# Stick breaking with features on the partitions: one product turned round, the outputs' transposes left out

## What is computed

```
u = rmsnorm(x) @ w_in            # queries qb, keys kb, values vb, gate zb: 1024 columns each
z = (q @ k^T) / sqrt(128)        # per head, per block of 128 queries, keys up to the block
log_1mb = where(s < t, log_sigmoid(-z), 0)
A = where(s < t, exp(log_sigmoid(z) + sum over s < j < t of log_1mb), 0)
hb = A @ v
yb = hb * silu(zb)
y = concat(ya, yb) @ w_out       # ya: the mLSTM branch
x = x + rmsnorm(y)
```

## Time and profile before

| | |
|---|---|
| median of 3 runs | 1892.0 us |
| lowest, highest | 1891.76, 1892.29 us |
| profiled execution, own time | 1892.71 us |
| its span | 1890.7 us |
| mean granted TensorE clock | 0.999 of full speed |
| TensorE busy in the span | 99% |

### The profile page before, as it was taken

The page is one execution under the profiler, slowest core; times in us unless marked ns, Lnnn a source line. Parts: engine busy times, 40 slices in busy tenths (PEclk is TensorE's granted clock), DMA queues, the critical chain, the costliest instruction groups (busy, mean ns, idle before and its releaser), DMA issues.

```text
span 1890.7 us, 25969 instructions
## 1 busy us (share of the span) xinstructions
PE 1877.7 (99%) x9298; PEld 1589.8 (84%) x9298; DVE 1000.3 (53%) x1489; ACT 899.3 (48%) x1737; POOL 1043.7 (55%) x1265
## 2 busy tenths in 40 slices
PE   9999999999999999999999999999999999999998
PEld 7878888898888988888889888888878888998887
DVE  2531321431123398777737864876546748854652
ACT  5522443532333454455555544276646756653332
POOL 5732644453465498878854753166524364565572
PEclk9999999999999999999999999999999999999999
DMA  6341533232233432233242331569522244733331
GB/s 238 103 110 43 136 84 89 73 87 75 78 106 106 146 100 90 90 111 109 74 146 62 105 96 45 134 173 273 127 62 68 95 140 121 192 102 94 95 117 50
DMA packets 112626, 205.52 MB, mean 109 GB/s; under 512 B 11612, under 2 KB 17352, under 8 KB 112510
## 3 DMA queue, kind: packets, MB, share of 16 engines
q1 hardware_dynamic: 97684, 176.70, 31.0%
q0 software_dynamic: 6912, 12.59, 4.1%
q10 hardware_dynamic: 7914, 14.69, 2.3%
HBM read 195.80 MB, written 8.12 MB: 108 GB/s over the span
## 4 chain that ended last, share of the span: by engine, by line
PE 96%; DVE 2%; ACT 1%; DMA 0%; issue 0%; POOL 0%; DVEq 0%; SPq 0%; ACTq 0%; POOLq 0%
PE proj L2664 22%; PE proj L2666 21%; PE proj L2665 21%; PE work L3100 2%; PE work L3102 2%; PE work L3101 2%; PE proj L2822 2%; PE proj L2821 2%; PE proj L2823 2%; PE proj L2815 1%; PE proj L2817 1%; PE proj L2818 1%; PE work L3262 1%; PE work L2666 1%; PE work L2665 1%; PE work L2664 1%
## 5 line engine op out<-in xcount | busy, mean ns | idle before, releaser
L788 POOL TENSOR_TENSOR w_lo<-w_raw,w_hi 128x256 fp32r<-128x256 f32 x1008 | 821.4, 850 | 684.5 <-ACT w_hi L862 683.9
L862 ACT CAST w_hi<-w_raw 128x512 fp32r<-128x512 f32 x552 | 326.4, 619 | 402.1 <-PE proj L2666 309.0
L2664 PE MATMUL proj<-act_hi,w_hi 128*128 128x512 f32 (+1 forms) x1184 | 446.9, 377 | 0.6 <-DVE arena L1970 0.3
L2666 PE MATMUL proj<-act_hi,w_lo 128*128 128x512 f32 (+1 forms) x1184 | 440.7, 372 | 0.0
L2665 PE MATMUL proj<-act_lo,w_hi 128*128 128x512 f32 (+1 forms) x1184 | 440.5, 372 | 0.0
L2664 PEld LDWEIGHTS proj<-act_hi,w_hi 128*128 128x128 f32 x1184 | 223.1, 188 | 40.2 <-issue 0.7
L2665 PEld LDWEIGHTS proj<-act_lo,w_hi 128*128 128x128 f32 x1184 | 223.1, 188 | 39.1 <-issue 0.7
L2666 PEld LDWEIGHTS proj<-act_hi,w_lo 128*128 128x128 f32 x1184 | 222.9, 188 | 39.2
L2664 PE MATMUL proj<-w_hi,act_hi 128*128 128x512 f32 x512 | 203.8, 398 | 0.1
L788 POOL TENSOR_TENSOR w_lo<-arena,w_hi 128x256 fp32r<-128x256 f32 x188 | 174.6, 962 | 48.6 <-ACT w_hi L862 48.5
L2666 PE MATMUL proj<-w_hi,act_lo 128*128 128x512 f32 x512 | 200.1, 391 | 0.0
(11 more groups left out here) (436 smaller groups left out, 3259.1 us busy)
## 6 DMA issues: line engine op xcount, KB each, us to landing
w_raw<-in_w_in SPq DMA_DIRECT2D x154, 256.0 KB, 2.7
w_raw<-in_w_in_ab SPq DMA_DIRECT2D x130, 256.0 KB, 2.8
w_raw<-in_w_mlp SPq DMA_DIRECT2D x72, 256.0 KB, 2.9
arena<-in_w_mlp SPq DMA_DIRECT2D x28, 512.0 KB, 4.0
w_raw<-in_w_in_c SPq DMA_DIRECT2D x56, 256.0 KB, 2.9
arena<-in_w_in_ab SPq DMA_DIRECT2D x32, 256.0 KB, 4.3
w_raw<-in_w_out_ab SPq DMA_DIRECT2D x32, 256.0 KB, 2.6
w_raw<-in_w_out_c SPq DMA_DIRECT2D x32, 256.0 KB, 2.7
```

What stands on the lines that cost most here:

```text
L788: ins = pool.tensor_tensor(w_lo[:, slot, c], raw_of(b)[:, c], w_hi[:, slot, c].bitcast(F32), ALU.subtract)
L862: act.copy(w_hi[:, b % RING, :], raw_of(b)).then_inc(hi_ready, 1)
L2664: pe.matmul(out_, a_hi, b_hi, start=first, stop=False, skip_group_check=by_part)
L2666: return pe.matmul(out_, a_lo, b_hi, start=False, stop=last, skip_group_check=by_part)
```

## The change

- `sb_z` is computed with features on the partitions, as the odd layer's slabs are. Its quarters leave PSUM by VectorE (`rowed`: times the row of token scales), and ScalarE applies silu in place in SBUF to two banks at a time, waits for it and sends them to DRAM (`gate_spilled`), each a step later in ScalarE's program. The DRAM tensor is now feature by token.
- `values` has its operands swapped: its output has features on the partitions, and `sb_o` with it. The eight `turn_tile` and their waits go.
- `fill_hi` and `fill_lo` for the output's second half read `sb_o` in SBUF. ScalarE makes five of the eight in step 32 and three in step 33, VectorE seven in step 33 and the last behind the loop.
- `scores` waits, at the first unit of each head, for that head's keys alone.
- `GATED_AT` is one step later throughout.

```diff
--- before.py
+++ after.py
@@ -453 @@
...
-        sb_v, sb_o = [view(12288, MT, SEQ), view(14336, MT, SEQ)], view(0, MT, D)
+        sb_v, sb_o = [view(12288, MT, SEQ), view(14336, MT, SEQ)], view(0, KD, SEQ)
...
@@ -465 @@
...
-        gate_dram = nc.dram_tensor("gate_made", (SEQ, D), F32, kind="Internal").ap().rearrange("(m p) d -> p m d", p=P)
+        gate_dram = nc.dram_tensor("gate_made", (D, SEQ), F32, kind="Internal").ap().rearrange("(k p) t -> p k t", p=P)
...
@@ -1399 @@
 
             o_, spilled_, z_, v_ = even_sevens
 
-            def spill(quarter):
-                at, tokens, i = sevens.index(spilled_), (0, 2, 0, 2)[quarter], (0, 1, 1, 0)[quarter]
+            def gate_spilled(quarter):
+                at, half, i = sevens.index(spilled_), (0, 1, 0, 1)[quarter], (0, 1, 1, 0)[quarter]
+                slots = (late_gates if quarter > 1 else gate_tmp)[:, 2 * (quarter % 2):2 * (quarter % 2) + 2, :]
                 if quarter == 0:
                     act.wait_ge(a_out, 2 * at + 2)
                 elif quarter == 1:
                     act.wait_ge(own_out, 2 * at + 2)
                 else:
                     act.wait_ge(proj_free, spilled_.bank0 + 2 * (quarter - 2) + 2)
-                slot = 2 * (quarter % 2)
-                act.dma_start(gate_dram[:, tokens:tokens + 2, i * NCOL:(i + 1) * NCOL], (late_gates if quarter > 1 else gate_tmp)[:, slot:slot + 2, :])\
-                   .then_inc(dram_spilled, 16)
+                step(act.activation(slots, slots, ACT.Silu))
+                act.dma_start(gate_dram[:, 4 * i:4 * i + 4, 2 * P * half:2 * P * (half + 1)],
+                              slots.rearrange("p m (c t) -> p (m c) t", c=2)).then_inc(dram_spilled, 16)
...
@@ -1477 @@
             act.activation(root[:], stat[:], ACT.Sqrt, bias=eps_col[:, 0:1], scale=4.0 / D).then_inc(head_root_ready, 1)
             act.preload_act_table_set("silu_and_others")
             prepared_to(spilled_, B22, 3)
-            gate(spilled_, 0, ACT.Silu, None)
-            spill(0)
             prepared_to(spilled_, T4, 3)
-            gate(spilled_, 1, ACT.Silu, None)
-            spill(1)
+            gate_spilled(0)
             prepared_to(z_, B11, 3)
-            gate(spilled_, 2, ACT.Silu, None)
-            spill(2)
+            gate_spilled(1)
             prepared_to(z_, T1, 3)
-            gate(spilled_, 3, ACT.Silu, None)
-            spill(3)
+            gate_spilled(2)
             prepared_to(z_, T2, 3)
+            gate_spilled(3)
...
@@ -1547 @@
             def gates_back():
                 act.wait_ge(dram_spilled, 32 + 16 * 4)
                 act.wait_ge(sb_z_full, SB_UNITS // 2)
-                act.dma_start(first_gate, gate_dram[:, :, 0:NCOL]).then_inc(dram_returned, 16)
+                act.dma_start(first_gate, gate_dram[:, 0:4, :]).then_inc(dram_returned, 16)
                 act.wait_ge(sb_o_full, SB_UNITS // 2)
-                act.dma_start(sb_gate, gate_dram[:, :, NCOL:D]).then_inc(dram_returned, 16)
+                act.dma_start(sb_gate, gate_dram[:, 4:8, :]).then_inc(dram_returned, 16)
...
@@ -1564 @@
                     weights(i - 1)
                 if i == SB_UNITS // 2 + 2:
                     gates_back()
+                if i == SB_UNITS:
+                    fill_hi("act", ACT_AT["yb"], 5, src=sb_o, ready=(yb_ready, lambda k: k + 1), after=end("sb_k"))
+                if i == SB_UNITS + 1:
+                    fill_hi("act", ACT_AT["yb"], KD, src=sb_o, ready=(sb_o_copied, lambda k: MT * (k + 1)), k0=5)
                 for s, j in [x_ for later in beside[i:i + 3] for x_ in later]:
                     prepare(s.first + j + 1)
             ahead(by_name["even_out0"][1])
-            fill_hi("act", ACT_AT["yb"], 2, turn=TURN_AT["yb"], after=end("sb_k"))
             act.wait_ge(sb_o_copied, SB_UNITS)
             for r in range(2):
                 act.dma_start(post_row[r], bass.AP(W["post_norm_g_2"].tensor, r * D, [[0, P], [1, D]]))\
                    .then_inc(rows_loaded, 16)
             act.dma_start(pre1_row, bass.AP(W["pre_norm_g_2"].tensor, D, [[0, P], [1, D]])).then_inc(rows_loaded, 16)
-            fill_hi("act", ACT_AT["yb"], KD, turn=TURN_AT["yb"], k0=2, beside=by_name["even_out1"][0])
+            first = by_name["even_out1"][0]
+            prepare(first.first + first.n + KD - 3)
...
@@ -2418 @@
             rests(g_, T3, 3)
             c_from_b(g_)
             head_scales(2)
+            def rowed(quarter):
+                s, half, sign = g_, (0, 1, 0, 1)[quarter], (1.0, -1.0, -1.0, 1.0)[quarter]
+                for m in range(2):
+                    if quarter == 0:
+                        wait_product(vec, s, B21, m)
+                        src, sem_ = work[:, m, :], a_out
+                    elif quarter == 1:
+                        vec.wait_ge(own_summed, 2 * sevens.index(s) + m + 1)
+                        src, sem_ = s.own[:, m, :], own_out
+                    else:
+                        wait_product(vec, s, (B22, T4)[quarter - 2], m)
+                        src, sem_ = proj[:, 2 * (quarter - 2) + m, :], proj_free
+                    slot = (late_gates if quarter > 1 else gate_tmp)[:, 2 * (quarter % 2) + m, :]
+                    r_ = sb_r_row[:, 2 * P * half:2 * P * (half + 1)].unsqueeze(1).to_broadcast([P, 2, 2 * P])
+                    vec.scalar_tensor_tensor(slot.rearrange("p (c t) -> p c t", c=2), src.rearrange("p (c t) -> p c t", c=2), sign, r_,
+                                             ALU.mult, ALU.mult).then_inc(sem_, 1)
+
             rests(g_, B22, 3)
+            rowed(0)
             rests(g_, T4, 3)
             own_from_b(g_)
             rests(z_, B11, 3)
+            rowed(1)
+            rowed(2)
             rests(z_, T1, 3)
+            rowed(3)
             rests(z_, T2, 3)
...
@@ -2462 @@
...
+            def natural_(m):
+                return slice(m * P, (m + 1) * P)
+
             GATED_FROM = 5 * SB_UNITS // 8
-            GATED_AT = (21, 22, 25, 26, 29)
+            GATED_AT = (22, 23, 26, 27, 30)
 
             def output(u):
                 h, blk = u // MT, u % MT
-                o_ = sb_o[:, blk, h * HD:(h + 1) * HD]
+                o_ = sb_o[:, h, natural_(blk)]
                 vec.wait_ge(sb_o_full, u + 1)
                 if u < GATED_FROM:
                     ins = vec.tensor_copy(o_, work[:, 3, 0:HD])
                 else:
-                    ins = vec.tensor_tensor(o_, work[:, 3, 0:HD], sb_gate[:, blk, h * HD - NCOL:(h + 1) * HD - NCOL], ALU.mult)
+                    ins = vec.tensor_tensor(o_, work[:, 3, 0:HD], sb_gate[:, h - 4, natural_(blk)], ALU.mult)
                 ins.then_inc(sb_o_copied, 1)
 
             def gated(i):
@@ -2480 @@
                     vec.wait_ge(dram_returned, 16 * 3)
                 if i < MT:
                     vec.wait_ge(sb_o_copied, SB_UNITS // 2)
-                    o_, gate_ = sb_o[:, i, 0:NCOL], first_gate[:, i, :]
+                    o_, gate_ = sb_o[:, i, :], first_gate[:, i, :]
                 else:
                     vec.wait_ge(sb_o_copied, GATED_FROM)
-                    o_, gate_ = sb_o[:, :, NCOL:NCOL + HD], sb_gate[:, :, 0:HD]
+                    o_, gate_ = sb_o[:, MT, :], sb_gate[:, 0, :]
                 vec.tensor_tensor(o_, o_, gate_, ALU.mult).then_inc(yb_ready, 1)
 
             def first_half_out(name, i):
@@ -2510 @@
                         keys(1)
                     elif s is by_name["even_out0"][0]:
                         first_half_out("even_out0", 0)
-            fill_lo("act", ACT_AT["yb"], 2, turn=True)
+                if i == SB_UNITS + 1:
+                    fill_lo("act", ACT_AT["yb"], 7, src=sb_o)
+            fill_lo("act", ACT_AT["yb"], KD, src=sb_o, k0=7)
             first_half_out("even_out0", 1)
 
             def layer_out(name, first, second):
-                if name == "post0":
-                    fill_lo("act", ACT_AT["yb"], KD, turn=True, k0=2)
-                else:
+                if name == "post1":
                     pool_mixed(3)
                     fill_lo("aux", AUX_AT["mixb"], KD, src=odd_z[:, KD:2 * KD, :])
...
@@ -2783 @@
...
-                features, left_at = s in odd_sevens, LEFT_ODD if s in odd_sevens else LEFT_EVEN
+                features, left_at = s in odd_sevens or s.name == "sb_z", LEFT_ODD if s in odd_sevens else LEFT_EVEN
...
@@ -3235 @@
 
             def scores(u):
                 half, h, nk = u // 16, u % 16 // MT, (u % MT + 1) * P
-                if u % 16 == 0:
-                    pe.wait_ge(proj_free, by_name["sb_k"][half].end)
+                if u % MT == 0:
+                    pe.wait_ge(proj_free, by_name["sb_k"][half].bank0 + h + 1)
                 if u >= 2:
                     pe.wait_ge(sb_t, u - 1)
                 pe.matmul(work[:, u % 2, 0:nk], sb_q[half][:, h, natural(u % MT)], sb_k[half][:, h, 0:nk],
@@ -3259 @@
                 if u:
                     pe.wait_ge(sb_o_copied, u)
                 for kb in range(n_):
```

(15 more changed lines are left out.)

## The result

The changed kernel takes 1895.41 us (median of 22 runs, 1893.83 to 1897.90), the kernel before 1892.34 (22 runs, 1891.74 to 1894.94): a ratio of 1.0015, 95% interval 1.0009 to 1.0021. Measured once more later (11 runs against 21) it was 1894.14 against 1892.61, 1.0009 [1.0000, 1.0018]. So it is slower by 1.5 to 3 us, within the 0.2% that the forecast called no change. It lies 1.7 to 3 us above the forecast's point, outside the narrower band of 1891.0 to 1893.6 that was given 0.55, and the first comparison's 1895.41 stands at the very edge of the range (1895.4). Ratios leave out the few executions of any kernel that took 2077 us or more.

The account below looks back on a forecast made before the run. TensorE, busy 1877.7 of 1890.7 us, was taken to bound the kernel. The terms +2.2 - 1.0 + 0.6 + 1.9 + 0.5 - 3.7 made +0.5 us, a median of 1892.4, no change; range 1889.6 to 1895.4.

Parts of the forecast that it names:

- `sb_z`'s form: TensorE in `sb_z`: 336 matmuls of 256 columns instead of 168 of 512 cost +2.2 us, bounds 2.1 to 2.4.
- the gates' way out: `sb_z`'s quarters leaving PSUM by VectorE, silu in SBUF on ScalarE: cost 0, at most 2 us if a hand-over is late.
- first scores: Start of the first scores: waiting for the first head's keys alone saves 1.0 us, bounds -1.1 and -0.5.
- gate product into step 25's path: The moved product delays VectorE's copies and `output(22)`, so TensorE's wait in step 25 grows +0.6 us, bounds 0 and +1.3.
- casts ahead of `weights_copied(31)`: Five ScalarE casts in step 32 delay `values(31)` by +1.9 us, TensorE standing 2.4 us; bounds +1.0 and +2.6.
- late first weights of `even_out1`: VectorE's seven subtractions in step 33 delay `even_out1[0]`'s first weights, TensorE waiting +0.5 us; bounds 0 and +3.3.
- rival D: TensorE's clock falls after the 2.4 us without work, losing 1.7 us: 1894.1 us; chance 0.04.
- transposes: Transposes of the output tiles on TensorE at the loop's end fall away: -3.7 us, bounds -3.5 and -4.0.
- Rival B: All seven VectorE subtractions take 1.2 us, so TensorE waits 3.3 us for `even_out1[0]`'s first weights: 1895.2 us; chance 0.12.
- A: Rival: the loop's end costs TensorE nothing, the +1.9 and +0.5 fall away: 1890.0 us; chance 0.18 with ways to it.
- C: Rival: the quarters' new way out of PSUM is late, TensorE waits 2 us at an `sb_z` hand-over: 1894.4 us; chance 0.06.

Follow-up runs that it names:

- experiment 4: Changed kernel with only TensorE's form of `sb_z` put back to 168 matmuls of 512 columns (output then differs): 1892.84 us, 0.9997 of the kernel before.
- Kernel 8: Changed kernel with gate products back one step and the loop's end reordered (casts behind the weight casts, VectorE's seven behind the loop): 1890.26 us, ratio 0.9987.
- experiments 1: Changed kernel with the five gate products back in steps 21, 22, 25, 26 and 29: 1893.45 us, 1.0003 of the kernel before.
- experiment 3: Changed kernel with 18 idle transposes put into the hole ahead of `values(31)`: 1895.04 us, 1.0009 of the kernel before.
- 7: Changed kernel with the gate products back one step and 18 idle transposes ahead of the last `values`: 1893.26 us, 1.0002 of the kernel before.
- experiment 2: Changed kernel with ScalarE's five casts moved from step 32 to step 33, behind `weights_copied(31)`: 1894.26 us, 1.0007 of the kernel before.
- Experiment 6: Kernel before with one edit, the first half's five gate products one step later: 1894.16 us, ratio 1.0007.

## Why the prediction was right or wrong

The sum was +0.5; the stretch says +1.9. Term by term:

| term | forecast | measured |
|---|---|---|
| `sb_z`'s form | +2.2 | +2.2 (2.23 in its stretch, 2.25 in experiment 4) |
| the gates' way out | 0 | 0 (experiment 4) |
| first scores | -1.0 | -1.0 |
| gate product into step 25's path | +0.6 | +1.1 |
| casts ahead of `weights_copied(31)` | +1.9 | +1.7 |
| late first weights of `even_out1` | +0.5 | 0 at the low clock, 0.6 without it |
| clock behind the hole (rival D) | not in the sum | +1.55 |
| transposes | -3.7 | -3.6 |

The transposes are measured from the start of `values(31)` to TensorE's wait at 1592.14 us before, 1596.41 after: 65.18 us before, 63.11 after, of which 1.55 is the clock's. The measured terms make +1.95, the stretch +1.92. Kernel 8 gives -3.56 over the same way.

That the verdict, no change, held is owed to the width of its 0.2%, 3.8 us: the point was missed by more than the whole sum. Five of the seven terms of the sum were right to 0.2 us. **The step that failed is rival D**, given 0.04. Its working was right in kind (1.7 forecast, 1.55 measured) and its weighing wrong. Against it stood that the waits of the earlier trace rows leave the clock at full speed, but the longest of these is 0.9 us, and the hole that I forecast was 2.4; the only row with a longer wait was the run's start, and there the clock did fall. The row nearest to the forecast hole spoke for the rival. In the loop the clock fell behind all four holes of 2.2 us (the changed kernel twice, experiments 1 and 4), behind neither of the two that were filled (3 and 7), and behind one of six waits of 1.9 us in step 25 (experiment 2). The length of a wait does not decide it alone. At the run's start the clock fell behind waits of 1.86 us (the kernel before) and 2.12 us (the changed kernel), and stayed at 1.00 behind waits of 1.75 us (the changed kernel, its first) and 2.19 us (experiment 3). What else decides stays open, so a fair chance for D was well above 0.04 and below 1.

**The step-25 term was mis-sized**: +0.6 for one product of 0.68 us. The edge of my range, +1.3, came from the product itself being slow; it was not, the scan behind it was (0.42 to 0.90 us). A moved instruction shifts everything behind it, and one of those slid behind the start of a subtraction of GpSimd's. The rule of the Trainium skill, GPSIMD Engine Reference, section Specifications, that GpSimd and VectorE contend when a VectorE instruction has two SBUF inputs, agrees with it: the scan has two, and the instructions of the same steps with one input in PSUM keep their 0.29 us in both traces. Experiment 6 shows the same pair without the rest of the change.

Lying beside GpSimd's work is not enough, though; it matters which of the two started first. The scan of the next step, 128 x 256 with both inputs in SBUF, overlaps GpSimd's subtractions in both kernels. Before, it starts 0.02 us ahead of one:

```profile
1500.32 0.69 DVE L2462 TENSOR_TENSOR_SCAN arena<-carry,arena 128x256 f32<-128x256 f32 x1
1500.34 2.35 POOL L788 TENSOR_TENSOR w_lo<-w_raw,w_hi 128x256 fp32r<-128x256 f32 x2 [2.53 <-ACT w_hi L862]
```

After, it starts inside a pair of them:

```profile
1503.83 1.41 POOL L788 TENSOR_TENSOR w_lo<-w_raw,w_hi 128x256 fp32r<-128x256 f32 x2 [2.39 <-ACT w_hi L862]
1504.53 1.25 DVE L2484 TENSOR_TENSOR_SCAN arena<-carry,arena 128x256 f32<-128x256 f32 x1
```

In the first case the scan takes the 0.69 us that it takes alone, and GpSimd's two subtractions, behind it and a gate product, take 2.35; in the second the scan takes 1.25 and the two subtractions 1.41. So the later starter pays. The twelve traces bear this out from 1390 to 1560 us: 366 scans and products of 128 x 512 in SBUF started with no subtraction running, and all kept their own time to 0.01 us, the 172 into which a subtraction then fell as well; 41 started with a subtraction running that had 0.3 us or more to go, and all took longer, by 0.13 to 0.15 us less than the rest of it.

**The late weights** were right as a mechanism and hidden by the clock; without the fall they are a wait of 0.6 us (experiments 3 and 7), forecast 0.5. VectorE's string of seven took 6.43 us, 0.92 each, where I had three at 1.2 and four at 0.68, 0.90 on the mean. Rival B, with all seven long, did not occur; A did not either, and C is excluded: TensorE doesn't wait in `sb_z` or `lstm_z`.

**The level.** The first comparison has 3.07 us between the medians, 1.1 more than the stretch gives, the second 1.53, 0.4 less. The run's start differs by up to 3 us from one profile to the next (1218.87 to 1221.98 at the stage's start), also between kernels that are the same up to there. The first comparison's executions also had the lower clock: the mean over the 22 is 0.9976, over the 11 of the second 0.9983. By an estimate from these two numbers, 0.0006 of 1893 us or 1.2 us, more falls of the clock make most of the 1.5 us between the two comparisons; the first profile has one more than the second, at 18.8 to 22.2 us. Why it fell more often there stays open.

## What to carry to other kernels

A conversion that removes work from the busiest engine (here 3.6 us of transposes) can be lost by where the replacing work is queued: five casts ahead of the one copy that the idle engine waits for cost 1.7 us and a fall of TensorE's clock, the same casts behind it and behind the next weights cost nothing. With the gate products back in both, the ratio goes from 1.0003 to 0.9987. When a forecast contains a hole in TensorE's work, add what the clock costs behind it, by the row whose idle time is nearest to the hole's length, and give it more than a token chance. When an instruction is moved ahead of a queue that is just in time, price what the shift puts behind the start of another engine's work, not only the instruction.

## What the runs showed of the hardware

- TensorE's clock fell from 2.4 to 1.2 GHz behind a hole of 2.2 us in a stage that was busy before and after it, four times in four (experiments 1 and 4, the changed kernel twice); the matmuls of 512 columns then took 0.63 us instead of 0.39 for some 3 us. The loss, 1.5 us over two blocks, is nearly as large as the hole. With the hole filled by idle transposes the granted clock was 1.00, twice in two (experiments 3 and 7). At the run's start it fell behind waits of 1.86 and 2.12 us and not behind 1.75 and 2.19.
- Behind waits of 1.9 us in the loop it fell once in six (experiment 2).
- A scan of 128 x 128 with both inputs in SBUF takes 0.42 us, and 0.90 where a subtraction of GpSimd's started 0.11 us ahead of it. A scan of 128 x 256 that started 0.02 us ahead of the subtraction kept its 0.69 us, and the two subtractions, behind it and a gate product, took 2.35 us instead of the 1.41 that such a pair took where it had started first.
- Filling a hole and reordering what caused it are not the same: with the gate products back in both, the stretch is 665.30 us filled and 662.73 reordered.
